# A head norm's squares summed by four products of rounded operands, and the steps of the norm set anew by chunk

## The reference, cut to what matters

```python
h = rmsnorm(x, norm_g[l])
proj = h @ w_in[l]
(a_val, a_gate, a_z, q, k, v, b_z, c_b, c_c, c_x, c_z, gates) = jnp.split(proj, SPLIT_IDX, axis=-1)
...                                    # convolution branch: y_a
o = diff_attention(qh, kh, vh, lam)    # per head: (softmax(q1 k1) - lam * softmax(q2 k2)) v
o = rmsnorm(o, subln_g[l], SUBLN_EPS) * (1.0 - lam_init)
y_b = (o.reshape(b, s, W_B) * jax.nn.silu(b_z)) @ w_b_out[l]
...                                    # short convolution branch: y_c
merged = g[:, :, 0] * y_a + g[:, :, 1] * y_b + g[:, :, 2] * y_c
x = x + merged @ w_o[l]
return rmsnorm(x, final_g)
```

## Time and profile before

| | |
|---|---|
| median of 3 runs | 2284.86 us (2284.36 to 2284.91) |
| span of the profiled execution, first to last instruction | 2281.1 us |
| what lies around the span, against the median | 3.8 us |
| PE busy | 2257.2 us, 99% of the span, 10822 records |
| weight loads (PEld) busy | 1832.9 us, 80% |
| DVE busy | 1426.0 us, 63%, 2706 instructions |
| ACT busy | 756.0 us, 33%, 1610 instructions |
| POOL busy | 232.8 us, 10% |
| chain that ended last, PE's share | 96% |

### The profile page before, as it was taken

One profiled execution on the slowest core, in us unless ns is written; L12 is line 12 of the kernel. 1 busy time (PEld: TensorE's weight loads), 2 busy tenths in 40 slices (PEclk: granted clock), 3 DMA queues, 4 the chain that ended last, 5 costly groups with the idle time before them and its releaser, 6 DMA issues.

```text
span 2281.1 us, 29046 instructions
## 1 busy us (share of the span) xinstructions
PE 2257.2 (99%) x10822; PEld 1832.9 (80%) x10822; DVE 1426.0 (63%) x2706; ACT 756.0 (33%) x1610; POOL 232.8 (10%) x186
## 2 busy tenths in 40 slices
PE   7999999999999999999999999999999999999998
PEld 6888888878888888888788788888877787788886
DVE  4767667764666665564557667665556657677752
ACT  4333332342333331032344344102135455441121
POOL 3544400100000000010000000001000000000010
PEclk9999999999999999999999999999999999999999
DMA  8877788798566665566755565556765555545555
GB/s 315 288 265 265 270 289 290 273 342 321 166 203 183 181 175 183 190 254 238 263 185 170 166 199 156 169 196 239 257 258 144 179 161 168 156 136 183 187 193 201
DMA packets 99339, 493.53 MB, mean 216 GB/s; under 512 B 15360, under 2 KB 18304, under 8 KB 54144
## 3 DMA queue, kind: packets, MB, share of 16 engines
q1 hardware_dynamic: 90464, 488.90, 63.8%
q10 hardware_dynamic: 8736, 2.78, 0.6%
HBM read 378.37 MB, written 113.27 MB: 216 GB/s over the span
## 4 chain that ended last, share of the span: by engine, by line
PE 96%; DVE 2%; DMA 1%; issue 1%; ACT 0%; SPq 0%; DVEq 0%; ACTq 0%
PE PJ L769 75%; PE SC L828 6%; PE SC L860 5%; PE TB L869 3%; PE OB L893 1%; PE OB L894 1%; PE OB L828 1%; PE PJ L828 1%; PE OB L896 1%; PE OB L895 1%; PE TB L904 0%; DMA Wraw<-w_stream 0%; DMA PX<-x_t 0%; PE TB L920 0%; PE SC L769 0%
## 5 line engine op out<-in xcount | busy, mean ns | idle before, releaser
L769 PE MATMUL PJ<-hT,Wp 128*128 128x512 f32 x6480 | 1571.4, 394 | 0.5 <-DVE PX L1632 0.5
L769 PEld LDWEIGHTS PJ<-hT,Wp 128*128 128x128 f32 x6480 | 1189.5, 188 | 254.0 <-issue 17.7
L1552 DVE SCALAR_TENSOR_TENSOR ACCS<-UA,col,ACCS 128x512 f32<-128x512 f32 x464 | 350.7, 798 | 0.4
L1066 ACT ACTIVATE PX<-SC,negm 128x512 f32<-128x512 f32 (+3 forms) x320 | 196.2, 623 | 145.5 <-DVE negm L1381 143.6
L1426 DVE TENSOR_TENSOR ZA<-TB,ZA 128x512 fp32r<-128x512 f32 (+1 forms) x144 | 95.1, 660 | 177.0 <-ACT ZA L1086 176.0
L1381 DVE TENSOR_REDUCE negm<-SC 128x2 f32<-128x1024 f32 (+3 forms) x160 | 169.0, 1061 | 40.3 <-PE SC L860 37.6
L1086 ACT ACTIVATE ZA<-TB 128x512 fp32r<-128x512 f32 (+1 forms) x144 | 82.6, 574 | 321.8 <-PE TB L869 321.8
L1137 ACT ACTIVATE TG<-PJ,col 128x512 f32<-128x512 f32 x64 | 44.1, 690 | 351.2 <-PE PJ L769 351.2
L1419 DVE SCALAR_TENSOR_TENSOR PX<-PX,sc 128x512 f32<-128x512 f32 (+3 forms) x160 | 108.0, 695 | 51.0 <-ACT PX L1077 50.8
L828 PE MATMUL SC<-Wp,KM 128*128 128x512 f32 x384 | 121.5, 389 | 0.0
L1077 ACT ACTIVATE PX<-PX,sc 128x512 f32<-128x512 f32 (+3 forms) x160 | 98.9, 655 | 64.9 <-DVE sc L1408 44.6
(11 more groups left out here) (192 smaller groups left out, 2037.4 us busy)
## 6 DMA issues: line engine op xcount, KB each, us to landing
Wp<-split_weights SPq DMA_DIRECT2D x264, 1024.0 KB, 4.8
split_weights<-Wp SPq DMA_DIRECT2D x88, 1024.0 KB, 4.9
Wraw<-w_stream SPq DMA_DIRECT2D x88, 512.0 KB, 5.9
KM<-keys SPq DMA_DIRECT2D x24, 512.0 KB, 5.9
VM<-values SPq DMA_DIRECT2D x24, 512.0 KB, 6.5
PX<-x SPq DMA_DIRECT2D x16, 512.0 KB, 7.6
out<-PX SPq DMA_DIRECT2D x16, 512.0 KB, 10.6
keys<-KM SPq DMA_DIRECT2D x12, 512.0 KB, 9.5
```

The lines of the kernel that those rows point to most:

```text
L769: mm = pe.matmul(pj(c, r)[:, :], wt, rhs[:, 1 if q == 1 else 0, k, :], start=(n == 0), stop=(n == 3 * ktiles - 1))
L1066: a = act.activation(probs(c, h, t, j, m)[:, 0:w], SC[k][:, m, 0:w], ACT.Exp, bias=negm[:, t % 2, j, m:m + 1], accum_out=lsum[:, t % 2, j, ...
L1552: a = dve.scalar_tensor_tensor(out=acc, in0=src, scalar=col[:, n:n + 1], in1=acc, op0=ALU.mult, op1=ALU.add)
```

## The change

The squares are no longer multiplied as plain float32. ACT squares as before and then copies the squares, rounded, into `SQ[:, 0]`; DVE subtracts the rounded half from the squares into `SQ[:, 1]` (the new helper `o_square_lo`); TensorE sums with two products for each tile, one of the rounded half and one of the rest, both with a rounded column of ones that is two columns wide. `sum_squares` now waits for DVE instead of ACT. The causal mask is held once instead of twice. And nearly every constant of the step tables has another value.

```diff
-SCORE_SPAN = 55
+SCORE_SPAN = 56
-MAX_LAG = (1, 1, 1, 1)
-EXP_LAG = (2, 2, 2, 2)
+MAX_LAG = (1, 1, 1, 0)
+EXP_LAG = (2, 2, 2, 1)
...
-CLAMP_LAG = (6, 6, 6, 6)
-OSQ_LAG = (7, 7, 7, 7)
-OSUM_LAG = (10, 10, 10, 9)
-OVAR_LAG = (11, 11, 11, 10)
+CLAMP_LAG = (6, 6, 8, 7)
+OSQ_LAG = (7, 6, 7, 7)
+OSQLO_LAG = (7, 9, 9, 8)
+OSUM_LAG = (14, 14, 10, 11)
+OVAR_LAG = (14, 15, 11, 10)
...
             def sum_squares(c, h, q):
-                squares = pair_rooms(c)[1]
-                pe.wait_ge(osq_done, pair_at(c, h, q) + 1)
+                pe.wait_ge(osq_lo, pair_at(c, h, q) + 1)
                 wait(pe, tb_free, TURN["o", c, h, q])
                 for i in range(2):
-                    mm = pe.matmul(TB[:, i:i + 1], squares[:, i * P:(i + 1) * P], onesf[:, 0:1], start=True, stop=True)
+                    for a in range(2):
+                        mm = pe.matmul(TB[:, 2 * i:2 * i + 2], SQ[:, a, i * P:(i + 1) * P], onesr[:, :],
+                                       start=(a == 0), stop=(a == 1))
                 mm.then_inc(osum_done, 1)
...
             def o_square(c, h, q):
-                act.activation(squares, squares, ACT.Square, scale=OSCALE).then_inc(osq_done, 1)
+                act.activation(squares, squares, ACT.Square, scale=OSCALE).then_inc(act_square, 1)
+                act.wait_ge(act_square, pair_at(c, h, q) + 1)
+                act.activation(SQ[:, 0, :], squares, ACT.Copy).then_inc(osq_hi, 1)
...
+            def o_square_lo(c, h, q):
+                dve.wait_ge(osq_hi, pair_at(c, h, q) + 1)
+                dve.tensor_tensor(SQ[:, 1, :], pair_rooms(c)[1], SQ[:, 0, :].bitcast(F32), ALU.subtract
+                                  ).then_inc(osq_lo, 1)
...
             def o_var(c, h, q):
-                dve.tensor_scalar(ost[:, 3, :], TB[:, 0:2], FLT_MAX * OSCALE ** 2, None, ALU.is_le)
-                dve.tensor_scalar(ost[:, 1, :], TB[:, 0:2], FLT_MAX * OSCALE ** 2, None, ALU.min).then_inc(tb_free, 1)
+                dve.tensor_scalar(ost[:, 3, :], TB[:, 0:4:2], FLT_MAX * OSCALE ** 2, None, ALU.is_le)
+                dve.tensor_scalar(ost[:, 1, :], TB[:, 0:4:2], FLT_MAX * OSCALE ** 2, None, ALU.min).then_inc(tb_free, 1)
```

More of the change, by code:

```diff
@@ L176 @@
 SCORE_AT = 17
-SCORE_SPAN = 55
-MAX_LAG = (1, 1, 1, 1)
-EXP_LAG = (2, 2, 2, 2)
[L182 to L188, removed]
+SCORE_SPAN = 56
+MAX_LAG = (1, 1, 1, 0)
+EXP_LAG = (2, 2, 2, 1)
+MAX_ODD = (-17, -5, -3, -1)
+EXP_ODD = (-16, -4, -1, 1)
+WDIFF_LAG = (3, 3, 3, 1)
+WEXP_LAG = (4, 4, 3, 2)
+SUM_LAG = (4, 7, 5, 3)
+SCALE_LAG = (5, 6, 4, 4)
+COMB_LAG = (8, 7, 7, 6)
 TURN_LAG = (12, 11, 10, 10)
@@ L193 @@
 HI_LAG = (0, 0, 0, -1)
-LO_LAG = (1, 1, 1, 0)
-PV_LAG = (4, 4, 4, 4)
-OCOPY_LAG = (5, 5, 5, 5)
-CLAMP_LAG = (6, 6, 6, 6)
-OSQ_LAG = (7, 7, 7, 7)
-OSUM_LAG = (10, 10, 10, 9)
-OVAR_LAG = (11, 11, 11, 10)
[L202 to L213, removed]
+LO_LAG = (1, 1, 2, 0)
+PV_LAG = (5, 4, 4, 4)
+OCOPY_LAG = (3, 5, 5, 5)
+CLAMP_LAG = (6, 6, 8, 7)
[3 more added lines that the diff above has]
+OVAR_LAG = (14, 15, 11, 10)
+OPOW_LAG = (12, 15, 11, 11)
+OSCALE_LAG = (14, 17, 13, 11)
+STORE_LAG = (2, 19, 14, 15)
+BACK_LAG = (-2, 24, 21, 24)
+ZB_LAG = (0, 30, 30, 32)
+ZBHI_LAG = (0, 31, 30, 33)
+ZBLO_LAG = (0, 32, 30, 36)
+DIRECT_SPREAD = (24, 18, 16, 15)
+DIRECT_ZB = (22, 17, 17, 16)
+DIRECT_HI = (23, 18, 18, 17)
+DIRECT_LO = (25, 18, 19, 18)
 Q_LO_AT = 3
-K_LO_AT = 1
+K_LO_AT = 2
 Z_AT = 1
@@ L219 @@
 VLO_AT = 44
-ZCHI_AT = 69
+ZCHI_AT = 67
 ZCLO_AT = 70
 LN_AT = (408, 408, 408, 414)
-LN_CENTER_AT = 2
+LN_CENTER_AT = 1
 LN_SQ_AT = 3
-LN_ADD_AT = 5
-LN_VAR_AT = 10
+LN_ADD_AT = 3
+LN_VAR_AT = 9
 LN_POW_AT = 10
@@ L234 @@
 ZA_HI_AT = 23
-ZA_LO_AT = 24
+ZA_LO_AT = 23
 X_LOAD_AT = (436, 440)
@@ L469, in build @@
         onesn = sb("onesn", [P, P])
-        mask = sb("mask", [P, 2, P])
+        mask = sb("mask", [P, 1, P])
         col = sb("col", [P, COLS])
@@ L487, in build @@
         nhalf = sb("nhalf", [P, 4])
+        onesr = sb("onesr", [P, 2], F32R)
+        SQ = sb("SQ", [P, 2, 2 * P], F32R)
         lnst = sb("lnst", [P, 5, NT])
@@ L522, in build @@
         t_done, at_hi, tb_free = sem("t_done"), sem("at_hi"), sem("tb_free")
-        pv_done, ob_free, o_ready, osq_done = sem("pv_done"), sem("ob_free"), sem("o_ready"), sem("osq_done")
+        pv_done, ob_free, o_ready, act_square = sem("pv_done"), sem("ob_free"), sem("o_ready"), sem("act_square")
+        osq_hi, osq_lo = sem("osq_hi"), sem("osq_lo")
         osum_done, ovar_ready, opow_done, on_ready, o_spread, zf_ready = (
@@ L1176, in _ @@
             split_hi(2)
+            act.wait_ge(const_pool, 2)
+            act.activation(onesr[:, :], onesf[:, 0:2], ACT.Copy)
             act.wait_ge(col_in, 16)
@@ L1287, in _ @@
                                pattern=[[-1, P]], channel_multiplier=1).then_inc(const_pool, 1)
-            for m in range(2):
-                ins = pool.affine_select(out=mask[:, m, :], in_=mask[:, m, :], compare_op=ALU.is_ge, fill=MASKED, base=0,
-                                         pattern=[[-1, P]], channel_multiplier=1)
-            ins.then_inc(const_pool, 1)
+            pool.affine_select(out=mask[:, 0, :], in_=mask[:, 0, :], compare_op=ALU.is_ge, fill=MASKED, base=0,
+                               pattern=[[-1, P]], channel_multiplier=1).then_inc(const_pool, 1)
             for t in range(NT):
@@ L1377, in max_unit @@
                 if j == c:
-                    dve.tensor_tensor(SC[k][:, :, w - P:w], SC[k][:, :, w - P:w], mask[:, :, :], ALU.add
+                    dve.tensor_tensor(SC[k][:, :, w - P:w], SC[k][:, :, w - P:w], mask[:, :, :].to_broadcast([P, 2, P]), ALU.add
                                       ).then_inc(masked, 1)
@@ L1731, in _ @@
                         split_lo(p // PARTS + 2)
+                    for u in pairs_at(c, p - OSQLO_LAG[c]):
+                        o_square_lo(c, *u)
                     for u in pairs_at(c, p - OVAR_LAG[c]):
```

## The result

| | before | after |
|---|---|---|
| median | 2284.44 us of 8 runs (2283.68 to 2284.91) | 2290.11 us of 8 runs (2288.60 to 2291.63) |
| ratio | | 1.0025, 95% interval 1.0016 to 1.0034 |
| span of the profiled execution | 2281.1 us | 2289.8 us (its own time 2291.63) |

The change makes the kernel slower by 0.25%, 5.7 us. The execution that was profiled is the slowest of its eight, 1.5 us above their median. Its own time less its span leaves 1.8 us (2291.63 and 2289.8), and not the 3.8 us put around the span ahead of the prediction; by that the profiled execution of the kernel before was some 2 us faster than its median, an estimate. So the two spans differ by 8.7 us where the medians differ by 5.7.

What follows compares the result with a forecast made beforehand. PE, busy 99% of the span, was taken as the bound. Products 0, interruptions -0.8, `o_var` wait -0.4, tight turns +0.2 gave -1.0 us: span 2280.1 plus 3.8 is 2283.9 us; 8-in-10 range 2279.5 to 2290.5.

Steps and rivals of the forecast that it cites:

- the 3.8 us put around the span: Whole kernel: time outside the profiled span, 3.8 us, added to the forecast span of 2280.1 us to give 2283.9 us.
- Rival D: Chunk 1: ACT's standstill reaches PE if a store lands 14 us or more after issue; +10, 2294 us; chance 0.06.
- The products: Sum of squares on PE: four rounded products cost what the four float32 records did, 0; ends -2.9 and +3.8 us.
- Rival C: Sum of squares on PE: short rounded products cheaper than their loads, 2275.9 us, half of that 2280; chance 0.13.
- Fewer interruptions: PE's list: short groups interrupt the projections 382 times instead of 390; -0.8 us, from -0.5 to -1.4.
- Work added beside PE: 32 rounded copies on ACT and 32 subtractions on DVE, 0.42 us each, are covered by PE; 0.
- `TB` handed on: Bank handovers after moved steps: chunk 3's wait behind `o_var` goes, -0.4 us; tight turns over the chunks, +0.2 us.
- Rival B: `TB` comes free too late in chunk 2, behind `turned_lo`: 2289.5 us, with chunk 3 up to 2294; chance 0.13.
- The scale's way through memory: Chunk 1, `load_scales`: ACT stands still 1 to 4 us in most of 7 pairs, covered by ten steps; 0 on PE.

Runs made afterwards that it cites:

- the tables alone: Changed kernel with its step tables but the float32 sum of before, no rounded copy or subtraction: 2288.97 us, ratio to before 1.0023.
- the run with half of them: Against the changed kernel with intermediate norm and scale-use lags in chunk 1 (2283.00 us), the sum takes only the rounded half of the squares: 2276.10 us.
- The tables with chunk 1's norm as before: Changed kernel's tables with the float32 sum of before, and chunk 1's norm lags set back to those before: 2284.46 us, ratio 1.0000.
- the link alone: Kernel before with its own tables, only the split sum (copy, subtraction, four rounded products) and single mask added: 2302.80 us, ratio 1.0084.
- one user left behind: Split sum on the tables of before, chunk 0's sum, o_var, power and scale moved later, the scale's spread left at lag 19: 2298.21 us.
- all moved: Split sum on the tables of before, chunk 0's sum, o_var, power and scale later, spread at 24, its use at 24 to 26: 2288.44 us, ratio 1.0018.

## Why the prediction was wrong

It forecast 2283.9 us, 1.0 us faster than before, and no change that can be measured; the kernel is 5.7 us slower. 2290.1 lies inside the range, by 0.4 us, but above the 2289.4 up to which the prediction called it no change. The rival nearest to what happened (D) had a chance of 0.06. Step by step:

- **The products, 0.** Right. 0.47 us a pair before and 0.46 after; the tables alone lose the time without them; and the run with half of them confirms the pace that the sum rests on, 0.11 us a load. Rival C, products cheaper than their loads, doesn't occur.
- **Fewer interruptions, -0.8.** Not shown. The tables with chunk 1's norm as before run like the kernel before (1.0000, 0.9991 to 1.0009, which is too wide to tell 0.8 us).
- **Work added beside PE, 0.** Right for the change, as its own waits show. But the cover isn't free: on the tables of before the same work costs 18.8 us, through a chain that was looked at for chunk 2 alone.
- **`TB` handed on, -0.4 and +0.2.** The -0.4 is wrong: the wait behind `o_var` is still there, 0.5 us. Rival B doesn't occur: PE has no wait behind `turned_lo` in chunk 2.
- **The scale's way through memory, 0 on PE.** This step failed; by PE's late starts in chunk 1 it is +5.6 us in the profiled execution, and by the medians of the tables with and without chunk 1's norm 4.5 us. It says "ACT will stand still for 1 to 4 us in most of the 7 pairs", and "ten steps, 9 us, less 3 us for that work itself, cover it". ACT stood for up to 8.3 us: from the store's issue to the moment when ACT came to the load there were 5.3 to 6.0 us in six pairs and 1.7 us in the seventh, not 7 to 8, and the store's landing took 8.8 to 11.2 us in chunk 1. And the cover was counted for one kind of pair. Where the load is at step 24 of a head's first pair, the next thing on ACT is the `turned_hi` of step 26, with its product at 30: six steps, not ten. Above all the step follows ACT's list only. The load's landing has a waiter of its own, `zb_pair` on DVE, which the change moves two steps forward while the scale comes later. Neither `ZB_LAG` nor the time that the load takes to land entered the sum. In chunk 1 that is 5.0 to 7.2 us before and 5.1 to 9.0 after, with medians of 5.4 and 7.4.
- **Rival D** named the way over ACT, with a price of 10 us. Its point of decision, a store that lands 14 us after its issue, is wrong: 9.5 us did it where the store was late itself, and 10 us were enough on the way over DVE.

## What to carry to other kernels

Where a transfer is moved, list every waiter of its landing on every engine and subtract the measured landing from the new room, pair by pair; the engine that issues it is one of several. When a chain gets a link more, move all of its users, for a single one that is left behind can keep most of the price (18.8 us with the link alone, 14.2 us with one user left behind, 4.4 us with all moved). And an edit that gives nothing alone may be half of a cure: where two waits in parallel end at the same product, only the runs with one, the other and both tell it.
